# Latent heads in pairs on column halves, differential heads with fp32r scores and later turns

## The reference, cut to what matters

```
def _softmax_attention(q, k, v, scale):      # latent: 8 heads, q and k of 96, v of 64
    s = einsum('bhqd,bhkd->bhqk', qb, k) * scale
    return einsum('bhqk,bhkd->bhqd', softmax(s), v)

def _diff_attention(q1, q2, k1, k2, v, lam, scale):   # 8 heads, q and k of 64 twice, v of 128
    p1 = softmax(einsum(qa, k1) * scale)
    p2 = softmax(einsum(qb, k2) * scale)
    return einsum('bhqk,bhkd->bhqd', p1 - lam * p2, v)
```

## Time and profile before

| | us |
|---|---|
| median of 3 runs | 1848.85 (1846.56 to 1856.86) |
| the profiled execution, its own time | 1855.64 |
| its span, first to last instruction | 1853.8 |
| long units of the latent heads | about 496 to 594 |
| long units of the differential heads | about 1265 to 1386 |

### The profile page before, as it was taken

One profiled execution on the slowest core, in us unless ns is written; L12 is line 12 of the kernel. 1 busy time (PEld: TensorE's weight loads), 2 busy tenths in 40 slices (PEclk: granted clock), 3 DMA queues, 4 the chain that ended last, 5 costly groups with the idle time before them and its releaser, 6 DMA issues. The chain is left out here.

```text
span 1853.8 us, 23467 instructions
## 1 busy us (share of the span) xinstructions
PE 1459.9 (79%) x8491; PEld 1151.2 (62%) x8492; DVE 967.6 (52%) x1530; ACT 639.4 (34%) x1016; POOL 453.3 (24%) x210
## 2 busy tenths in 40 slices
PE   4799999656999998188993199989997862988870
PEld 1688888555577445166772199987884442766750
DVE  0412122276377252645775835418994755646558
ACT  1311212242344111155773412115552121746543
POOL 1000000112000032335775500010000232645556
PEclk8899999877899999589997599999998885999995
DMA  8576754701000810357995032220005322867863
GB/s 273 177 238 210 245 183 160 173 12 31 1 1 1 278 76 24 136 206 279 387 388 203 23 94 69 70 62 10 1 1 173 136 97 84 326 255 289 310 222 142
DMA packets 125055, 280.10 MB, mean 151 GB/s; under 512 B 12441, under 2 KB 64369, under 8 KB 112657
## 3 DMA queue, kind: packets, MB, share of 16 engines
q1 hardware_dynamic: 113984, 239.15, 37.3%
q0 software_dynamic: 10096, 36.33, 5.7%
q10 hardware_dynamic: 864, 3.15, 0.4%
HBM read 248.99 MB, written 34.85 MB: 153 GB/s over the span
## 5 line engine op out<-in xcount | busy, mean ns | idle before, releaser
L489 PEld LDWEIGHTS psum<-exact 128*128 128x128 f32 x3360 | 411.0, 191 | 57.8 <-issue 57.8
L489 PE MATMUL psum<-exact 128*128 128x258 f32 (+1 forms) x3360 | 421.0, 286 | 23.9 <-PEq L331 23.9
L1925 PE MATMUL psum<-exact,exact 128*128 128x512 f32 x912 | 222.3, 399 | 1.4 <-issue 0.9
L1925 PEld LDWEIGHTS psum<-exact,exact 128*128 128x128 f32 x912 | 171.9, 191 | 46.6 <-issue 8.7
L807 PE MATMUL psum<-higher 128*128 128x512 f32 x400 | 174.0, 595 | 2.7 <-PEq L733 2.7
L575 DVE COPY lower<-psum 128x258 f32<-128x258 f32 (+1 forms) x70 | 29.7, 424 | 239.6 <-PE psum L489 239.6
L807 PEld LDWEIGHTS psum<-higher 128*128 128x128 f32 x400 | 75.8, 191 | 95.5 <-issue 94.0
L2077 DVE TENSOR_TENSOR exact<-higher,exact 128x2048 fp32r<-128x2048 f32 x40 | 107.3, 2681 | 48.1 <-ACT exact L2022 48.1
L1299 ACT ACTIVATE higher<-psum,higher 128x640 f32<-128x640 f32 (+1 forms) x120 | 84.3, 706 | 119.7 <-DVE higher L1245 119.7
L533 ACT COPY lower<-psum 128x258 f32<-128x258 f32 (+1 forms) x70 | 26.1, 373 | 287.3 <-PE psum L489 287.3
L1202 PE MATMUL psum<-higher 128*128 128x320 f32 (+1 forms) x384 | 116.3, 440 | 5.0 <-PEq L1392 1.7
(11 more groups left out here) (307 smaller groups left out, 2392.3 us busy)
## 6 DMA issues: line engine op xcount, KB each, us to landing
higher<-in_moe_w SPq DMA_DIRECT2D x50, 1024.0 KB, 8.4
higher<-in_ada_w SPq DMA_DIRECT2D x48, 1024.0 KB, 5.2
lower<-in_moe_w SPq DMA_DIRECT2D x46, 1024.0 KB, 8.1
y_rows<-higher SPq DMA_DIRECT2D x32, 512.0 KB, 4.8
higher<-in_ev_w_in SPq DMA_DIRECT2D x15, 1032.0 KB, 7.7
higher<-in_od_w_in SPq DMA_DIRECT2D x11, 1024.0 KB, 5.2
lower<-mod_rows SPq DMA_DIRECT2D x16, 512.0 KB, 8.9
higher<-in_ev_w_out SPq DMA_DIRECT2D x4, 1536.0 KB, 12.2
```

Source lines behind the costliest of these rows:

```text
L489: last = T.matmul(bank(g % W_BANKS)[:, 0:cw], a, b[:, k], start=(k == 0 and m == 0), stop=(k == KD - 1 and m == 2))
L1925: last = T.matmul(bank(2), a[:, k, :], w, start=(k == 0 and m == 0), stop=(k == KD - 1 and m == 2))
```

## The change

`heads_attention` is replaced by two functions, `latent_heads` and `difference_heads`.

In `latent_heads` the values of two units (heads 2p and 2p + 1 of a tile) are computed together: for each key tile one matmul to rows 0 to 63 and one to rows 64 to 127 of the same bank, and one output copy of 128 rows for the pair. TensorE's list becomes `score(u + 1)`, then for odd u from 3 the values of the pair of units u - 3 and u - 2, then `turn(u - 1)`. VectorE copies two of the five turned tiles, ScalarE three. `pT` has four places in place of two.

In `difference_heads` queries and keys are split in a high and a low fp32r part, and each score half is the sum of three matmuls over 64 rows (rows 0 to 63 for the first softmax, 64 to 127 for the second), not padded. TensorE's list is `score(u)`, `turn(u - 2)`, `values(u - 3)`. ScalarE alone copies the turned weights, all five tiles in one instruction. `e_buf` has six places in place of four. The block ahead lets ScalarE write the high part of each of the 16 items and VectorE the low part after it; the zeros by GpSimd go.

The retention stage's GpSimd list gets a drain at its end. The latent output moves to another place in SBUF (`MLA_OUT`).

```diff
@@ retention, GpSimd
                         nc.gpsimd.tensor_tensor(g, g, cens[:, t % 2], ALU.mult).then_inc(gated, 1)
+                    pool.drain()
@@ latent_heads, TensorE
+                    def values(p):
+                        pe.wait_ge(c_d, 2 * p + 2)
+                        pe.wait_ge(c_a, min(2 * p + 2, LONG))
+                        if p >= 2:
+                            pe.wait_ge(put_s, p - 1)
+                        out = bank(6 + p % 2)
+                        for n, kt in enumerate(tiles[2 * p]):
+                            for r in range(2):
+                                u = 2 * p + r
+                                last = T.matmul(out[MDV * r:MDV * (r + 1), 0:P], value(units[u][1], kt), pT[:, u % 4, n, :],
+                                                start=(n == 0), stop=(n == len(tiles[u]) - 1))
+                        last.then_inc(valued, 1)
+                    score(0)
+                    for u in range(U + 2):
+                        if u + 1 < U:
+                            score(u + 1)
+                        if pair_at(u):                  # u % 2 == 1 and u >= 3
+                            values((u - 3) // 2)
+                        if 1 <= u <= U:
+                            turn(u - 1)
@@ latent_heads, VectorE
+                    top(0)
+                    for u in range(U + 2):
+                        if 1 <= u <= U:
+                            mix(u - 1)
+                        if u + 1 < U:
+                            top(u + 1)
+                        if pair_at(u):
+                            out((u - 3) // 2)
+                        if 1 <= u <= U:
+                            copy_p(u - 1)               # tiles 0 and 1
@@ latent_heads, ScalarE
+                    exps(0)
+                    for u in range(U + 2):
+                        if 1 <= u <= U:
+                            copy_p(u - 1)               # tiles 2 to 4
+                        if u + 1 < U:
+                            exps(u + 1)
@@ difference_heads, TensorE
+            PRODUCTS = ((0, 0), (0, 1), (1, 0))
+                    def score(u):
+                        t, h = units[u]
+                        for s in range(2):
+                            if u:
+                                pe.wait_ge(expd, 2 * u - 1 + s)
+                            for a in range(1 if t == 0 else 2):
+                                for m, (x, y) in enumerate(PRODUCTS):
+                                    out, k0, n = (view(s, 1), NT * P, P) if t == 0 else (view(s, NT)[:, a], a * HK, HK)
+                                    last = T.matmul(out, qT(t, h, s, x), kT(h, s, y, k0, n), start=(m == 0), stop=(m == 2))
+                            last.then_inc(scored, 1)
-                    for u in range(U + 2):
+                    for u in range(U + 3):
                         if u < U:
                             score(u)
-                        if u >= 2:
-                            values(u - 2)
-                        if 1 <= u <= U:
-                            turn(u - 1)
+                        if 2 <= u <= U + 1:
+                            turn(u - 2)
+                        if u >= 3:
+                            values(u - 3)
@@ difference_heads, VectorE
+                    for u in range(U + 3):
+                        if u < U:
+                            top(u)
                         if 1 <= u <= U:
                             mix(u - 1)
+                        if u >= 3:
+                            out(u - 3)
@@ difference_heads, ScalarE
+                        A.copy(pT[:, u % 2, 0:n], bank(4, 2)[:, 0:n * P].rearrange("p (n q) -> p n q", n=n)).then_inc(copied, 1)
+                    for u in range(U + 4):
                         if u < U:
                             exps(u)
+                        if 2 <= u <= U + 1:
+                            copy_p(u - 2)
+                        if u >= 4:
+                            square(u - 4)
@@ differential_attention, the block ahead
-                @block.gpsimd
-                def _(pool):
-                    for r in range(2):
-                        rows = slice(DDH * (1 - r), DDH * (2 - r))
-                        nc.gpsimd.memset(qT[rows, :, r, :], 0.0)
-                    pool.drain()
+                    for n, (kind, h) in enumerate(items):      # VectorE
+                        dve.wait_ge(ev_a, n + 1)
+                        src = bank(2 * (n % 4), 2)
+                        if kind == "k":
+                            V.tensor_tensor(kT[1][:, h, :], src[:, 0:NK * P], whole(kT[0][:, h, :]), ALU.subtract).then_inc(ev_d, 1)
+                        else:
+                            V.scalar_tensor_tensor(qT[1][:, h, :], src[:, 0:TOK], DIFF_SCALE, whole(qT[0][:, h, :]),
+                                                   ALU.mult, ALU.subtract).then_inc(ev_d, 1)
+                    for n, (kind, h) in enumerate(items):      # ScalarE
+                        act.wait_ge(tr, n + 1)
+                        src = bank(2 * (n % 4), 2)
+                        if kind == "k":
+                            A.copy(kT[0][:, h, :], src[:, 0:NK * P]).then_inc(ev_a, 1)
+                        else:
+                            A.mul(qT[0][:, h, :], src[:, 0:TOK], DIFF_SCALE).then_inc(ev_a, 1)
```

More of the change, by code:

```diff
@@ L1158, in _, with latent_heads @@
                         norm(t)
[L1160 to L1168, removed]
+        def latent_heads(units, qT, kT, value, e_buf, put, rsum, nmax, pT):
+            scored, maxed, expd = sem("mla_scored"), sem("mla_maxed"), sem("mla_expd")
+            mixed = sem("mla_mixed")
+            turned, c_a, c_d, valued, put_s = (sem(f"mla_{n}") for n in ("turned", "ca", "cd", "valued", "put"))
             U = len(units)
             tiles = [[NT] if t == 0 else list(range(NT)) for t, _ in units]
+            LONG, ND = sum(len(kt) > 1 for kt in tiles), 2
             def view(b, nk):
@@ L1191, in score @@
                         t, h = units[u]
[L1192 to L1203, removed]
+                        if u >= 2:
+                            pe.wait_ge(expd, u - 1)
+                        if t == 0:
+                            T.matmul(view(u % 2, 1), qT(t, h), kT(h, NT * P, P), start=True, stop=True).then_inc(scored, 1)
+                        else:
+                            for a in range(2):
+                                last = T.matmul(view(u % 2, NT)[:, a], qT(t, h), kT(h, a * KEYS // 2, KEYS // 2), start=True, stop=True)
+                            last.then_inc(scored, 1)
                     def turn(u):
@@ L1215, in turn @@
+                            last = T.transpose(bank(b)[:, c * P:(c + 1) * P], e_buf[:, u % 2, n * P:(n + 1) * P], ident)
                         last.then_inc(turned, 1)
[L1217 to L1220, removed]
-                        if u >= 2:
[L1222 to L1226, removed]
+                    def values(p):
[9 more added lines that the diff above has]
+                                                start=(n == 0), stop=(n == len(tiles[u]) - 1))
@@ L1239, in top @@
                     def top(u):
-                        for s in range(halves):
-                            v = halves * u + s
-                            nk = len(tiles[u])
-                            dve.wait_ge(scored, v + 1)
-                            src = view(v % 2, nk)
-                            V.tensor_reduce(nmax[:, v:v + 1], src, AX.X if nk == 1 else AX.XY, ALU.max,
-                                            negate=True).then_inc(maxed, 1)
+                        nk = len(tiles[u])
@@ L1291, in exps @@
                     def exps(u):
-                        for s in range(halves):
-                            v = halves * u + s
-                            nk = len(tiles[u])
+                        nk = len(tiles[u])
+                        act.wait_ge(maxed, u + 1)
+                        if u >= 2:
+                            act.wait_ge(turned, u - 1)
+                        A.activation(flat(u % 2, nk), view(u % 2, nk), ACT.Exp,
+                                     bias=nmax[:, u:u + 1], accum_out=rsum[:, 0, u:u + 1]).then_inc(expd, 1)
```

228 lines of the change are left out of this document (130 added, 98 removed).

## The result

The changed kernel takes 1828.8 us (median of 4 runs, 1827.88 to 1831.55) against 1851.69 for the kernel before: ratio 0.9872, 95% interval [0.9848, 0.9896]. In a later series on one chip, where it was run again, it took 1829.52 against 1855.36, ratio 0.9852 [0.9829, 0.9876]. The prediction was 1826, range 1813 to 1840, "faster".

What follows compares the result with a forecast made beforehand. TensorE's queue was taken to bound both attention stages. From the median 1848.85 us, +2.1 (drain), -18.6 and -1.0 (latent), +2.0 (block ahead) and -7.0 (differential), together -22.5, gave 1826 us, range 1813 to 1840.

Steps and rivals of the forecast that it cites:

- TensorE's queue bounds both stages: Both attention stages, long units: TensorE's own work sets the pace, 3.01 us a latent unit and 3.82 a differential one.
- the loop score - top - exp - second score: Differential long units: score, maximum, exponential and next score of one half take 2.9 us, so they keep up with 3.60.
- The halves of a latent pair run side by side: Latent values: matmuls on the two column halves overlap, 1.07 us plus 0.25 for mode changes, 1.3 a pair.
- A pair in 4.81 us: Latent long units: a pair repeats after 4.81 us, 2.41 a unit for 3.01, 18.6 us less over 31 distances.
- The short units' share, -1.0: Latent short units: one output copy for two and earlier scores give 1 us less over eight units.
- The drain, +2.1: End of retention: the latent block starts after GpSimd's last multiplication, not beside it, 2.1 us more, bounds 0 and 2.4.
- The block ahead, +2.0: Block ahead of the differential heads: VectorE writes a low part of all 16 items, 2.0 us more, bounds 1 and 4.
- Differential units, 3.60 us, -7.0: Differential long units: scores, changes, turn and values take 3.60 us in place of 3.82, 7.0 us less over 32 units.
- the line through the earlier trace: Differential scores: a line through fp32r matmuls of 258 and 512 columns gives 0.149 us for an instruction of 320.
- the second softmax's first matmul may run beside the first's last: 0.13 less: Differential scores: the two softmaxes stand on different 64 rows, so one matmul may overlap, 0.13 us less a unit.
- a rival's price: Differential heads: TensorE's bare sum without the changes' cost, and short units gain, 1815 us in all; chance 0.10.
- Differential heads, short units, 0: Differential short units: six score instructions for four, but maximum ahead of mix; no change, bounds 3 less, 4 more.

## Why the prediction was right, point by point

- *TensorE's queue bounds both stages.* Right for the kernel before. In the changed differential unit the loop score - top - exp - second score has joined it: the second half starts by its wait in 27 of 32 units, though this costs only 0.03 us a unit over what TensorE's list alone would give. The prediction had this loop at 2.9 us and passed it. It had taken one half by itself; the second half's maximum and exponential stand behind the first's, and its loop is 3.76 - 0.44 = 3.32 us, the whole unit.
- *The halves of a latent pair run side by side, 1.3 us for a pair's values with both changes.* Right: 1.24 with one change; undoing the order costs 10.7 us in the stage.
- *A pair in 4.81 us, 0.25 of it the wait for mix.* Measured 4.95. The wait was named rightly as what is late next: it is 0.26, and taking it away gives 0.30 a pair. The 0.14 too few are changes: turns take 0.60 and not 0.55, and the scores ahead of the values 1.17 and not 1.08. Long and short units together: -19.6 forecast, -18.1 measured (-16.5 in the repeat). The short units' share, -1.0, has the wrong sign: from the last long score on the stage takes 1.2 us more (0.7 in the repeat).
- *The drain, +2.1.* The gap grew by 2.4 us. Right, and shown in the stage alone; the whole time cannot tell.
- *The block ahead, +2.0.* Measured +1.6 in the profiled execution, +1.5 in that of the kernel with both softmaxes on the same rows, +2.1 to +2.8 in the eight others.
- *Differential units, 3.60 us, -7.0.* This is the term that was mis-sized: 3.32 and -13.0. It lies outside the prediction's own sign of being right (3.5 to 3.7 us a unit). An instruction costs what the line through the earlier trace rows gave, 0.148 against 0.149 (that line is 2.1 to 2.2 columns a ns by its own rows, 258 / 0.122 and 512 / 0.235, not near 2.4), and the changes cost about what was taken. The step that failed is "the second softmax's first matmul may run beside the first's last: 0.13 less". It is not one instruction but three (1.95 - 1.49 = 0.46 us, from the kernel with both on the same rows): so many were left of the first half when the second one started, by its wait and, 0.03 us before, by the order. The 3.32 us was in the text as a rival's price, for another reason (changes that cost nothing).
- *Differential heads, short units, 0.* From the last long score on the stage takes 1.3 us less (1.0 in the repeat); the long units alone gave 11.7 us (13.1).
- *The prediction missed a cost of the same part.* TensorE's clock falls to its lower level as the changed heads begin, where in the kernel before it stays at the upper one:

```profile
1236.80:1247.00 10.20, 6.98 (x55) 5.76 (x54) 9.29 (x13) 7.33 (x10) 0.00 (x0) 1.00 0.01 3
1247.00:1258.00 11.00, 8.81 (x41) 7.47 (x40) 6.09 (x11) 4.26 (x11) 0.00 (x0) 0.50 0.00 0
```
```profile
1255.00:1265.20 10.20, 7.75 (x55) 6.48 (x54) 6.60 (x10) 4.38 (x7) 0.00 (x0) 1.00 0.01 2
1261.00:1272.00 11.00, 8.72 (x37) 5.84 (x38) 7.32 (x14) 3.97 (x10) 0.00 (x0) 1.00 0.00 0
```

  (The first two rows are windows of the changed kernel, the others of the kernel before; the third number from the end is the granted clock.) The heads begin at 1246.8 and 1261.6. In the changed kernel the clock was at the upper level from 1236.8, TensorE was busy for 6.98 of 10.2 us, and the clock then stood at 0.50 from 1247.0 to 1264.1. In the kernel before it rose at 1255.0, TensorE was busy for 7.75 of the next 10.2 us, and it stayed up. All ten executions with the changed block ahead and heads have this fall, and none of the three with the old ones. That the sparser work of the new block is the cause fits this, but was not tested. The first four units take 3.59, 3.80, 3.93 and 5.99 us, 17.3 in place of 13.3 at 3.32 each (in the kernel before, at the upper clock, they take 15.0, no more than four at 3.82). By this estimate the clock costs 4 us here (2.6 in the repeat), and without it the stage would have given 17.
- *The sum.* 22.5 us forecast, 22.9 measured by the medians of the first series and 25.8 by those of the second. The closeness to the first is partly luck. By the stages the change gave 27.1 us, 4.6 more than forecast: the differential term was 6 us too small, and the latent one 1.5 too large. The profiled executions differ by 26.3, and the medians of the first series by less only because the kernel before scatters from 1846.56 to 1856.86 and its profiled execution stood 4 us above its median.

The Trainium skill (TensorEngine Tiling (Array Packing), Key Properties) has tiles of one mode work independently. In the changed heads the trace bears that out further than the prediction used it: the second half starts by its own wait, 0.05 us after it, with up to three instructions of the first half still to start.

## What to carry to other kernels

Where products use half of the rows or of the columns, put neighbours in the queue on different halves: alternating, two halves overlapped fully here (0.92 us for twelve instructions, 1.07 for twenty), one run behind the other only by three instructions. Then look at the wait of each half. Interleaving more finely is no gain when it makes both halves wait for the later one: it cost 0.43 us a unit here. After an engine's work shrinks, write down the loop that goes through the one place in PSUM, for the half that is served last, with its period; here it was 3.32 us, just over the 3.29 of TensorE's list. Test each part of a change by itself: the fp32r form was worth 2 to 4 us, the rest of the stage's gain came with row halves and later turns. The drain that the new memory layout asked for cost the whole length of the multiplication that it waits for, 2.4 us; another layout owed none.

## What the runs showed of the hardware that was not expected

- Float32 matmuls over 64 rows on different halves overlap nearly fully: eight of 320 columns in 1.19 us, against 2.16 over 128 rows. Three fp32r products were hardly better than one float32 product here (stretch 130 against 132).
- Two runs of matmuls on different halves, one run behind the other, overlap at their seam by three instructions, on columns (twenty in 1.78 us where one by one would be 2.14; the second run starts 0.71 us behind the first) as on rows (0.41 us behind).
- The granted clock stayed at 0.50 for 47.7 us with TensorE busy for 47.2 of it, in one execution; in the nine others with the changed heads it was back after 10 to 17 us.
